# A chain of eight transformer stages on one core: first loads, stage seams and FFN clamps in another order

## What is computed

```python
def first_block(x, mem, ...):
    for l in range(2):
        h = rms_norm(x, g_pre[l])
        u = h @ w_in[l]                       # 1024 x 3344, split into q, k, v, gates, ...
        oa = moba_attention(...) * silu(ga)   # 8 heads of 64
        ob = rms_norm(gla_attention(...), g_gla_out[l]) * silu(gb)
        mkv = rms_norm(mem, g_mem[l]) @ w_mem_kv[l]          # 1024 x 512
        om = mem_attention(...) * silu(gm)    # 4 heads of 64 over 256 memory tokens
        x = x + concat([oa, ob, om]) @ w_out[l]
    return x

def second_block(h, ...):
    for i in range(2):
        h = h + 0.5 * rms_norm_2(swiglu(rms_norm_2(h, g[0]), w_gate_up[i, 0], w_down[i, 0]), g[1])
        h = h + rms_norm_2(mixer_i(rms_norm_2(h, g[2])), g[3])   # i = 0: short convolution, i = 1: gated delta net
        h = h + 0.5 * rms_norm_2(swiglu(rms_norm_2(h, g[4]), w_gate_up[i, 1], w_down[i, 1]), g[5])
    return h

def swiglu(x, w_gate_up, w_down):             # 1024 x 5632, 2816 x 1024
    gate, up = jnp.split(x @ w_gate_up, 2, axis=-1)
    return (silu(gate) * up) @ w_down
```

## Time and profile before

| | |
|---|---|
| median of three executions | 1690.89 us |
| profiled execution: time | 1699.13 us |
| profiled execution: span from first to last instruction | 1697.1 us |
| PE busy | 1544.0 us (91%) |
| DVE, ACT busy | 1022.6 us (60%), 832.2 us (49%) |
| mean granted clock of TensorE | 0.966 |
| chain of waits that ended last | 70% PE, 11% DVE, 8% ACT, 5% issue, 3% DMA |
| 16 DMA engines, mean over the span | 141 GB/s |

### The profile page before, as it was taken

The page is one execution under the profiler, slowest core; times in us unless marked ns, Lnnn a source line. Parts: engine busy times, 40 slices in busy tenths (PEclk is TensorE's granted clock), DMA queues, the critical chain, the costliest instruction groups (busy, mean ns, idle before and its releaser), DMA issues.

```text
span 1697.1 us, 19025 instructions
## 1 busy us (share of the span) xinstructions
PE 1544.0 (91%) x7466; PEld 1262.6 (74%) x7466; DVE 1022.6 (60%) x1347; ACT 832.2 (49%) x1171; POOL 96.8 (6%) x171
## 2 busy tenths in 40 slices
PE   5899789998999999899999999886788899989997
PEld 4777668877888778788877888664577778778886
DVE  3766566755555566655656555556645556766564
ACT  4545462564444454554545445454545545554443
POOL 4000000000000000000000000001412221000000
PEclk9999989999999999999999999998989999999999
DMA  5433433334555454556554555341322212455552
GB/s 160 143 100 100 139 124 98 102 100 136 187 187 185 155 191 173 175 179 193 182 176 159 189 189 185 115 149 56 87 58 73 75 50 76 161 165 182 196 176 99
DMA packets 165712, 238.77 MB, mean 141 GB/s; under 512 B 19358, under 2 KB 112328, under 8 KB 165624
## 3 DMA queue, kind: packets, MB, share of 16 engines
q1 hardware_dynamic: 154336, 230.98, 41.5%
q0 software_dynamic: 1632, 5.41, 1.1%
q10 hardware_dynamic: 9656, 1.18, 0.4%
HBM read 235.96 MB, written 1.57 MB: 140 GB/s over the span
## 4 chain that ended last, share of the span: by engine, by line
PE 70%; DVE 11%; ACT 8%; issue 5%; DMA 3%; POOL 2%; ACTq 0%; SPq 0%; DVEq 0%; POOLq 0%
PE A L226 12%; PE A L227 11%; PE A L228 11%; PE G L226 4%; PE G L228 4%; PE G L227 4%; PE M L228 4%; PE M L226 4%; PE M L227 4%; DVE w_lo L210 3%; ACT w_hi L197 2%; PE G L968 2%; DVE gdn_gd_t L2321 2%; PE G L1010 1%; DMA raw<-in_w_mem_kv 1%
## 5 line engine op out<-in xcount | busy, mean ns | idle before, releaser
L210 DVE TENSOR_TENSOR w_lo<-raw,w_hi 128x2048 fp32r<-128x2048 f32 (+1 forms) x290 | 511.7, 1779 | 237.6 <-ACT w_hi L197 236.2
L197 ACT ACTIVATE w_hi<-raw 128x2048 fp32r<-128x2048 f32 (+1 forms) x290 | 424.7, 1483 | 199.2 <-DMA raw<-in_ffn_w_gate_up 138.6
L226 PE MATMUL A<-w_hi,x_hi 128*128 128x512 f32 (+1 forms) x640 | 276.3, 432 | 20.2 <-DVE x_lo L369 7.7
L227 PE MATMUL A<-w_lo,x_hi 128*128 128x512 f32 (+1 forms) x640 | 254.8, 398 | 0.0
L228 PE MATMUL A<-w_hi,x_lo 128*128 128x512 f32 (+1 forms) x640 | 254.6, 398 | 0.0
L226 PEld LDWEIGHTS A<-w_hi,x_hi 128*128 128x128 f32 x640 | 125.8, 197 | 54.5 <-issue 12.2
L228 PEld LDWEIGHTS A<-w_hi,x_lo 128*128 128x128 f32 x640 | 125.4, 196 | 27.3
L227 PEld LDWEIGHTS A<-w_lo,x_hi 128*128 128x128 f32 x640 | 126.1, 197 | 21.3 <-issue 2.5
L227 PE MATMUL A<-w_lo,ffn_ffn_hT_hi 128*128 128x512 f32 x352 | 140.2, 398 | 0.0
L226 PE MATMUL A<-w_hi,ffn_ffn_hT_hi 128*128 128x512 f32 x352 | 140.2, 398 | 0.0
L228 PE MATMUL A<-w_hi,ffn_ffn_hT_lo 128*128 128x512 f32 x352 | 138.6, 394 | 0.0
(11 more groups left out here) (357 smaller groups left out, 2303.5 us busy)
## 6 DMA issues: line engine op xcount, KB each, us to landing
raw<-in_ffn_w_gate_up SPq DMA_DIRECT2D x176, 512.0 KB, 4.7
raw<-in_ffn_w_down SPq DMA_DIRECT2D x88, 512.0 KB, 4.0
raw<-in_w_in SPq DMA_DIRECT2D x52, 512.0 KB, 4.5
raw<-in_gdn_w_in SPq DMA_DIRECT2D x48, 512.0 KB, 4.6
raw<-in_sc_w_in SPq DMA_DIRECT2D x24, 512.0 KB, 4.3
raw<-in_w_out SPq DMA_DIRECT2D x16, 512.0 KB, 4.6
raw<-in_gdn_w_out SPq DMA_DIRECT2D x16, 512.0 KB, 4.0
raw<-in_w_mem_kv SPq DMA_DIRECT2D x8, 512.0 KB, 8.3
```

The source lines that it names most:

```text
L197: ins = act.activation(net.w_hi[:, v % RING, part], net.raw[:, v % RING, part], ACT.Copy)
L210: ins = dve.tensor_tensor(net.w_lo[:, v % RING, part], net.raw[:, v % RING, part], net.w_hi[:, v % RING, part].bitcast(F32), ALU.subtract)
L226: pe.matmul(out, xh, hi[:, k, c, :], start=start and k == 0, stop=False)
L227: pe.matmul(out, xh, lo[:, k, c, :], start=False, stop=False)
```

## The change

- **Start.** SP loads half of mem, unit `mem 0`, the other half of mem, unit `mem 1`, then x's halves, each with a semaphore of its own; POOL no longer loads mem in block 0. The gains `g_mem` and `g_pre` go first, into a third side of `rows`, and only they are waited for; PE turns the other gains inside `xpre`. The splits of the first two units move into `mempre`: the first ahead of, the second behind the norm of mem.
- **Blocks.** `xpre` moves from `mem 0` to `mem 1`; `rms` is parted in `rms:mem` and `rms:x`, the latter behind `evac:mem`; `evac:b` instead of `evac:mem` waits for x's factor. `mempre` of block 1 becomes the step `nextmem` in block 0's last unit, between its second and third quarter, and behind `hi:1`. Two memsets of DVE move behind the unit `mem 1`.
- **Seams.** `Post.weigh` multiplies a bank by scale and gain in the bank itself, as soon as ACT has squared it; `add` is then one pass a bank, x = x + r * bank. Both first groups of the next norm are transposed after bank (1,0), the third and fourth together before the fourth quarter. The second look-ahead unit is split in halves: ACT's first half right after the first squares, DVE's first half before the products; the second halves after the first root, and after the tt 0 group of the next norm.
- **FFN.** `make_hidden` is parted in `clamp` and `gate`. In step 0 the clamp stands ahead of the second `split_lo`; in the last step clamp and gate stand ahead of the last `split_lo`, and the sigmoid ahead of the last `split_hi`. In the steps between, the order is as before.
- **Tail.** `out` is written in four parts of 256 KB.

```diff
     def last_units(self, post, parts):
...
-                    if n == len(parts) - 1 and tt == 1 and post.then is not None:
-                        if c == 1:
-                            mm.then_inc(net.unit_used, 1)
-                        post.then.turn(pe, c)
-                if tt == 1 and (n < len(parts) - 1 or post.then is None):
+                    if n == len(parts) - 1 and (tt, c) == (1, 0) and post.then is not None:
+                        post.then.turn(pe, 0)
+                        post.then.turn(pe, 1)
+                if tt == 1:
                     mm.then_inc(net.unit_used, 1)
...
     def first_units(self, pre, banks):
...
-                    if pre.joined and (tt, h, q) in ((0, 1, 0), (0, 1, 1)):
-                        pre.turn(pe, 2 + q)
+                    if pre.joined and (tt, h, q) == (0, 1, 1):
+                        pre.turn(pe, 2)
+                        pre.turn(pe, 3)
...
     def act(self, w):                    # Post
         w.split_hi()
         self.squares(w, 0, 0)
+        w.split_hi(0, self.half_split.sem)
         self.squares(w, 0, 1)
         self.root(w, 0)
-        w.split_hi()
+        w.split_hi(1)
+        if then is not None:
+            then.round(w, 0)
         self.squares(w, 1, 0)
         if then is not None:
-            then.round(w, 0)
             then.round(w, 1)
...
+    def weigh(self, dve, tt, c):
+        net, bank = self.net, self.net.A[2 * tt + c][:, :]
+        dve.wait_ge(*self.squared(2 * tt + c + 1))
+        dve.scalar_tensor_tensor(out=bank, in0=bank, scalar=self.scale, in1=net.brow[:, c * 512:(c + 1) * 512],
+                                 op0=ALU.mult, op1=ALU.mult).then_inc(self.scaled.sem, 1)
...
+            dve.scalar_tensor_tensor(out=cols, in0=net.A[2 * tt + c][:, :], scalar=net.post_r[:, tt:tt + 1],
+                                     in1=cols, op0=ALU.mult, op1=ALU.add).then_inc(self.x_ready.sem, 1)
...
     def dve(self, w):                    # Post
         w.split_lo()
-        self.add(w, 0)
-        if self.then is not None:
-            self.then.dve_tile(dve, 0)
-        w.split_lo()
-        self.add(w, 1)
-        if self.then is not None:
-            self.then.dve_tile(dve, 1)
+        w.split_lo(0, self.half_split(1))
+        dve.wait_ge(*self.loaded(16))
+        self.weigh(dve, 0, 0)
+        self.weigh(dve, 0, 1)
+        self.add(dve, 0)
+        if then is not None: ...             # gain 0, gain 1, rest 0, rest 1
+        w.split_lo(1)
+        self.weigh(dve, 1, 0)
+        self.weigh(dve, 1, 1)
+        self.add(dve, 1)
...
     def act(self, w):                    # Ffn, steps 1 and later
             w.split_hi()
             self.hid_hi(w, j - 1)
-            w.split_hi()
-            self.sigmoid(w, j)
             if j < self.steps - 1:
                 w.split_hi()
+            self.sigmoid(w, j)
+            w.split_hi()
...
     def dve(self, w):                    # Ffn
         w.split_lo()
+        dve.wait_ge(*self.pre.r_ready(1))
+        self.clamp(w, 0)
         w.split_lo()
-        dve.wait_ge(*self.pre.r_ready(1))
-        self.make_hidden(w, 0)
+        self.gate(w, 0)
         for j in range(1, self.steps):
             w.split_lo()
             self.hid_lo(w, j - 1)
-            w.split_lo()
-            self.make_hidden(w, j)
             if j < self.steps - 1:
                 w.split_lo()
+            self.clamp(w, j)
+            self.gate(w, j)
+            w.split_lo()
...
             mempre
-            mem 0 [ | xpre | | rms]
-            mem 1 [ | | | evac:mem]
+            mem 0 [ | | | ]
+            mem 1 [xpre | rms:mem | | evac:mem rms:x]
...
-                 "out:1:0:0 hi:0 out:1:0:1 hi:1 out:1:0:2 lo:0 out:1:0:3 lo:1 add:1".split()
+                 "out:1:0:0 hi:0 out:1:0:1 hi:1 nextmem out:1:0:2 lo:0 out:1:0:3 lo:1 add:1".split()
...
     def sp(self, w):                     # Block
             elif step[1] == "mem":
+                if self.prev is None:
+                    half = (slice(None), slice(None), slice(h * 512, (h + 1) * 512))
+                    w.eng.dma_start(self.cat[half], self.mem_dram[half]).then_inc(w.net.mem_halves[h], 16)
                 w.load([4, 512], cols(self.w_mem, (512 * h, 512 * h + 512), 0, 512))
...
     def dve(self, w):                    # Block, block 0 only
+                self.mempre.gain(dve, 0)
+                self.mempre.gain(dve, 1)
+                w.split_lo()
+                self.mempre.rest(dve, 0)
+                self.mempre.rest(dve, 1)
...
-            for c in range(2):
+            for n in range(4):
+                sp.wait_ge(*before[0](n + 1))
+                part = (slice(None), n // 2, slice(n % 2 * 512, n % 2 * 512 + 512))
+                sp.dma_start(out_t[part], net.x[part]).then_inc(net.out_done, 16)
...
         def _(act):
-            for dst, src in net.row_loads:
+            for dst, src in net.row_loads[1]:
+                act.dma_start(dst, src).then_inc(net.first_params, 16)
+            for dst, src in net.row_loads[0]:
                 act.dma_start(dst, src).then_inc(net.params, 16)
-            for _ in range(LEAD):
-                w.split_hi()
             act.wait_ge(net.rows_turned, 1)
```

More of the change, by code:

```diff
@@ L78, in __init__ @@
         self.x = self.sb("x", [P, TT, D])
+        with ExitStack() as start:
+            keep, self.ctx = self.ctx, start
+            self.rows = self.sb("rows", [P, 3, P])
+            self.ctx = keep
         self.x_hi = self.sb("x_hi", [P, KT, T], F32R)
@@ L106, in __init__ @@
         self.params = self.sem("params")
+        self.first_params = self.sem("first_params")
+        self.mem_halves = [self.sem(f"mem_in{c}") for c in range(2)]
         self.rows_clear = self.sem("rows_clear")
@@ L110, in __init__ @@
         self.consts = self.sem("consts")
[L111 removed]
+        self.x_halves = [self.sem(f"x_in{c}") for c in range(2)]
         self.out_done = self.sem("out_done")
@@ L199, in split_hi, with split_lo @@
             ins.then_inc(net.w_hi_ready, 1)
-    def split_lo(self, half=None):
+        elif half_done is not None:
+            ins.then_inc(half_done, 1)
+    def split_lo(self, half=None, half_ready=None):
         net, v, dve = self.net, self.u, self.eng
@@ new lines, in dve @@
+        dve.wait_ge(*self.loaded(16))
+        self.weigh(dve, 0, 0)
+        self.weigh(dve, 0, 1)
+        self.add(dve, 0)
+        if then is not None:
+            then.gain(dve, 0)
+            then.gain(dve, 1)
+            then.rest(dve, 0)
+            then.rest(dve, 1)
+        w.split_lo(1)
+        self.weigh(dve, 1, 0)
+        self.weigh(dve, 1, 1)
+        self.add(dve, 1)
+        if then is not None:
+            then.gain(dve, 2)
+            then.gain(dve, 3)
+            then.rest(dve, 2)
+            then.rest(dve, 3)
+            dve.wait_ge(*then.lo(4))
@@ L901, in pe @@
             kind = step[0]
-            if kind == "mempre":
-                if self.x_before is not None:
-                    pe.wait_ge(*self.prev.cat_lo(4))
-                pe.wait_ge(*self.mem_loaded(16))
-                self.mempre.pe(pe)
+            if kind == "mempre" and self.prev is None:
+                pe.wait_ge(net.mem_halves[0], 16)
+                self.mempre.turn(pe, 0)
+                self.mempre.turn(pe, 1)
+                pe.wait_ge(net.mem_halves[1], 16)
+                self.mempre.turn(pe, 2)
+                self.mempre.turn(pe, 3)
+            elif kind == "nextmem" and self.next is not None:
+                pe.wait_ge(*self.cat_lo(4))
+                pe.wait_ge(*self.probs(len(self.items)))
+                pe.wait_ge(*self.next.mem_loaded(16))
+                self.next.mempre.pe(pe)
             elif kind == "xpre":
                 pe.wait_ge(*self.mempre.gained(4))
+                if self.prev is None:
+                    pe.wait_ge(net.params, 16 * net.late_loads)
+                    for side in range(2):
+                        mm = pe.transpose(net.A[2][:, side * P:(side + 1) * P], net.rows[:, side, :], ident[:, :])
+                    mm.then_inc(net.rows_turned, 1)
                 self.xpre.pe(pe)
@@ L1076, in act @@
             kind = step[0]
-            if kind == "mempre":
+            if kind == "mempre" and self.prev is None:
+                w.split_hi()
                 self.mempre.act(w)
+                w.split_hi()
+            elif kind == "nextmem" and self.next is not None:
+                self.next.mempre.act(w)
             elif kind == "xpre":
+                if self.prev is None:
+                    act.wait_ge(net.rows_turned, 2)
+                    act.activation(net.cols[:, 0:2, :], net.A[2][:, 0:2 * P], ACT.Copy).then_inc(net.cols_ready, 1)
+                    act.wait_ge(net.cols_ready, 2)
                 self.xpre.act(w)
             elif kind == "rms":
-                self.mempre.act_r(w, self.r_mem)
-                self.xpre.act_r(w)
+                if step[1] == "mem":
```

(23 more changed lines are left out.)

101 lines of the change are left out of this document (47 added, 54 removed).

## The result

The changed kernel takes 1645.63 us (median of four, 1642.65 to 1646.52) against 1692.32 for the kernel before beside it (1689.63 to 1695.63): a ratio of 0.972, 95% interval 0.970 to 0.974. Measured a second time, later, the ratio was 0.9724 (0.9705 to 0.9744). It is 46.7 us faster; 40.9 and a time of 1650.0 were forecast.

A forecast was written before the change was run, and what follows sets the result against it. PE, busy 91%, bounds the kernel, so gains come only from its pauses, low-clock matmuls and the two ends; 9.0 + 6.0 + 3.5 + 6.2 + 8.4 + 5.8 + 2.0 = 40.9 off 1690.9 gives 1650 us, range 1638 to 1662.

The forecast's parts named there:

- FFN steps, 15.0: FFN transposes of h: earlier clamps remove PE's seven waits, 9.0 us in four last steps and 6.0 in three first steps.
- Rival (e): FFNs: the clamps are held by something else than the split, so 15 + 3.5 us stay; 1669 us, chance 0.04.
- Clock behind these pauses, 3.5: Low-clock stretches behind the FFN pauses: 7.0 us if all go, half taken, 3.5, with ends 0 and 7.0.
- rival (a): The clock: no low stretch disappears, 1654 us, chance 0.14; second end, all disappear, 1646, chance 0.08.
- Seams, 6.2: Five seams: second token half starts 1.45 us sooner, 1.25 x 5 with late loads counted; 6.2 us, bounds 0 and 9.
- Rival (b): Seams: the half split waits for its load and holds squares and root, nothing gained; 1656 us, chance 0.11.
- Weighing, 0.75 a pass: DVE's weighing into PSUM in the seams: 0.75 us a pass taken for a PSUM source, adding 0 to 0.15 each.
- Rival (f): Weighing in the bank is slow while PE writes neighbouring banks; kernel slower, 1716 us at 3 us extra each; chance 0.03.
- Start and block 0, 8.4: From the start to b's transposes in block 0: 54.9 us against 63.29, 8.4 us sooner.
- Rival (c): The start is load-bound: unit 0's load ends at 14.9 as before, `mem 0` at 19.8; 1655 us, chance 0.08.
- r's wait, 2.5, and z's, 2.2: In the blocks: `turn:rb` now stops PE for 2.5 us waiting for r, and behind it z for 2.2.
- Rival (d): Blocks: r's wait costs PE nothing beyond the 2.5 us it replaces; 1643 us, chance 0.05.

The follow-up runs named there:

- whole_unit: The changed kernel with a seam's second look-ahead unit split whole again, behind the first token half's rest: 1650.8 us, ratio 0.9755.
- turns_old: The changed kernel with the transposes of a seam one by one again: 1656.1 us, ratio 0.9784.
- gains_sp: The changed kernel with the 17 late gain loads issued by SP behind x's halves instead of by ACT: 1646.83 us, ratio 0.9723.
- late_weigh: The changed kernel with the weighings waiting for the root: 1648.6 us, ratio 0.9741.
- blocks_old: The kernel before with the changed kernel's FFN clamps, seams and tail, its start and blocks the old ones: 1661.24 us, ratio 0.9814.
- weigh_tmp: The changed kernel with the weighing written to the SBUF buffer instead of its bank, and the add reading it there: 1649.1 us, ratio 0.9748.
- both: The changed kernel with ACT's rounds of the next mem ahead of the half splits and the late gain loads issued by SP: 1642.77 us, ratio 0.9701.
- rounds_first: The changed kernel with ACT's four rounds of the next block's mem ahead of its two half splits ending block 0: 1644.02 us, ratio 0.9709.

## Why the prediction was nearly right, and where it was not

The time, 1650.0, was 4.4 us too high. Its terms one by one:

- **FFN steps, 15.0.** Right. In the last step h is complete at 560.52 and PE comes at 561.31, a cover of 0.8 (0.9 forecast). What was moved behind also fits: the lo part of h ends at 563.6, PE asks at 564.5, a cover of 0.9; 0.7 was forecast. Rival (e) is out: the clamp was held by the split alone.
- **Clock behind these pauses, 3.5.** Within what the runs allow, but probably too low. All four low stretches are gone: PEclk is 1.00 in all four FFNs in both profiles of the changed kernel, as in rival (a)'s second end. Putting the pauses back cost 22 less 15, so 7 with an interval of some 4. By the stages above, FFN 01, FFN 10 and FFN 11 got 6.9 us shorter than seams, waits and tail account for (0.4, 4.6 and 1.9). Both lie at the 7.0 that was halved. On the other side, 46.7 less the 42.6 that the marks give (15.0, the seams' 11.2, 14.4 and 2.0) leaves only 4.1, where the 14.4 is read from two single executions that scatter by some us. That the halved term came out so near is in part luck.
- **Seams, 6.2.** The term that was mis-sized: 11.2 (2.33 each, less 0.5 for the late loads, below). The restart was right, 2.78 after the transposes' start against 2.89 forecast (595.65 less 592.76). The step that failed is the next one, "x's third and fourth bank come at 600.6 and 601.35": the half split was left where the whole one had begun, at 597.35 in the old frame, though the working itself had just moved gain and rest forward. It begins at 575.12 + 21.38 = 596.50, so the third transposes come at 599.85, without the wait of 0.85, and the second half at 602.67 instead of 603.5. That is 0.83 a seam. The other 0.2 a seam was the late load at two seams. It came, where it was forecast, but at half the price: ACT's half split waits 0.58 and 0.51 us for its load ahead of FFN 01 and FFN 11, the squares and the root move back with it, and PE waits 0.25 and 0.24 ahead of its first transposes, 0.5 in all and not 1.0. The marks, which count from these transposes, don't hold it. The seam ahead of FFN 01 in the changed kernel:

```profile
663.01 1.06 ACT L206 ACTIVATE w_hi<-raw 128x1024 fp32r<-128x1024 f32 x1 [0.58 <-DMA raw<-in_ffn_w_gate_up]
...
667.46 1.31 PE L353 MATMUL G<-ident,x 128*128 128x128 f32 x8 [0.25 <-DVE x L484]
```

Rival (b), that it eats the gain, is out by this size. whole_unit and turns_old show which edits carry the gain.
- **Weighing, 0.75 a pass.** 0.69. The prediction took the 0.75 of a row for the price of a PSUM source; it was that of the scalar read from a column (last section). Rival (f) is out: 22 weighings beside PE's writes, none over 0.70 us.
- **Start and block 0, 8.4.** 8.1. ACT's issuing of the gain loads ended at 10.02, not 8.85: the same list took 1.2 us longer, which moved `mem 0` to 16.00 (14.9 forecast). L came at 31.3 instead of 30.4, and from L to b's transposes it was 23.9 instead of 24.5. r came 6.9 after L, 7.0 forecast. Rival (c) is out: ACT begins the split of unit 0 at 10.38 straight behind the copy, and in gains_sp, where it has to wait for the load, at 9.81, not at 14.9.
- **r's wait, 2.5, and z's, 2.2.** The sum was near (3.8 instead of 4.7 a block), the form wrong: instead of two waits in each block there are four, 1.19 for the bank of `y_mem`, 1.07 for r, 0.71 and 0.79 behind it. The evacuation behind mem's root holds b's first matmuls before r can hold anyone; the prediction had that evacuation in r's sum but not as a wait of its own. Since the chain to b's transposes runs through all of it, the total stood. Rival (d) is out.
- **Block 1, 5.8.** 6.3 (239.42 against 239.7 forecast). `mem 0` came at 200.63 instead of 201.65 because the load landed sooner.
- **Tail, 2.0.** 2.0: from PE's last matmul to the end of the span 7.5 us before and 5.4 after. late_weigh shows the 1.4 of it that are DVE's.

**What stays open.** How long the stretch ahead of the first seam and the gated delta net take differs by 3 to 4 us between executions with identical instructions; which small delay tips it was not found. The edits of start and blocks were put back only together (blocks_old), so their single worth rests on marks, and so does that of the four writes of `out`.

## What to carry to other kernels

When an engine's chain is moved forward, carry the new times through every later instruction on that engine: the mis-sized term was one split left at its old time. Of a bundle of edits at one place, take each back alone: here the conspicuous one (product ahead of the root) was worth nothing in the seams, and the order of the transposes most of it. A pause of PE can cost more than its length: in these traces those of 3.4 and 4.0 us brought a stretch at half clock, those of about 2 us sometimes did, and four of 0.7 to 1.3 us did not, so several short waits can be better than a long one with the same sum. Where an instruction waits for a load, look at what stands behind it in the same queue and doesn't need that load: moving ACT's rounds ahead took the pause between the blocks away.

## What the runs showed of the hardware

**What makes a DVE pass longer here is the scalar, not the bank.** Groups of 128x512 `scalar_tensor_tensor` and their mean ns, in the kernel before, the changed kernel and weigh_tmp (L466 and L484 take r from a column in SBUF, L470 and L475 a constant):

```profile
L466 DVE SCALAR_TENSOR_TENSOR tmp<-A,small,brow 128x512 f32<-128x512 f32 x24 | 17.9, 747 | 25.0 <-ACT small L438 25.0
L470 DVE SCALAR_TENSOR_TENSOR x<-tmp,x 128x512 f32<-128x512 f32 x24 | 16.6, 692 | 0.8
```

```profile
L484 DVE SCALAR_TENSOR_TENSOR x<-A,small,x 128x512 f32<-128x512 f32 x24 | 16.9, 747 | 1.4
L475 DVE SCALAR_TENSOR_TENSOR A<-A,brow 128x512 f32<-128x512 f32 x24 | 15.7, 691 | 6.4 <-ACT scratch L438 6.4
```

```profile
L484 DVE SCALAR_TENSOR_TENSOR x<-tmp,small,x 128x512 f32<-128x512 f32 x24 | 17.0, 749 | 1.4
L475 DVE SCALAR_TENSOR_TENSOR tmp<-A,brow 128x512 f32<-128x512 f32 x24 | 15.6, 683 | 6.5 <-ACT scratch L438 6.5
```

With r from a column a pass takes 747 to 749 ns whether its source is PSUM or SBUF; with a constant 683 to 692, from and to PSUM, from PSUM to SBUF, or within SBUF. The prediction read 0.75 against 0.69 as PSUM against SBUF and as agreeing with the Trainium skill ("Perfetto Trace Analysis", Optimizing Scalar/DVE Operations: some 125 ns of access overhead on PSUM, 60 on SBUF). The two rows of before differed in both respects at once, and the difference belongs to the other one; for passes of this size no run here shows the page's difference.

**The clock, and a slow pace that it doesn't show.** Behind pauses of 3.4 and 4.0 us PEclk was 0.50, so 1.2 GHz (1.11 us for four transposes instead of 0.60, 0.80 us for a matmul instead of 0.50). At the start PE comes to its full pace at about 20 us in both the changed kernel and gains_sp, though `mem 0` began at 16.00 and at 14.74; over all kernels with this start that moment lies between 17.9 (`both`) and 22.1 us (rounds_first). In the changed kernel PEclk shows most of that stretch low; in gains_sp it says 1.00 while 12 matmuls take 5.3 us:

```profile
16.00:20.00 4.00, 4.00 (x11) 3.14 (x12) 3.12 (x5) 2.78 (x3) 3.49 (x9) 0.59 0.70 238
```

```profile
14.70:20.00 5.30, 5.26 (x12) 4.13 (x13) 4.07 (x6) 3.43 (x5) 4.59 (x12) 1.00 0.91 264
```

So PEclk alone doesn't find all slow matmuls; their own durations (0.63 us against 0.39) do. The slow pace in gains_sp, a matmul each 0.43 us, is that of the changed kernel's stretch at half clock, so it may be that the clock was low there too and the record lacks it; that was not shown.
